# Hybrid decoder layer: output weights with folded gains, split during the projection and used in three rounded products, and attention maps normed behind the values

## What is computed

```python
h = rms_norm(x, norm1_g[l])
proj = h @ w_in[l]                                   # 512 x 3072
dq, dk, dv, rq, rk, rv, rg = jnp.split(proj, PROJ_SPLITS, axis=-1)
...
s = jnp.einsum('bqhmd,bkhmd->bhmqk', qb, k) * scale  # two maps m for each of 4 heads
s = jnp.where(causal, s, -jnp.inf)
p = jax.nn.softmax(s, axis=-1)
a = p[:, :, 0] - lam * p[:, :, 1]
out = jnp.einsum('bhqk,bkhd->bqhd', a, v)
...
d_out = rms_norm(d_out, diff_norm_g[l]) * (1.0 - lam_init)     # each head's 128 columns
r_out = rms_norm(retention(rq, rk, rv, log_decay), ret_norm_g[l])
r_out = r_out.reshape(B, S, RET_WIDTH) * jax.nn.silu(rg)
mix = jnp.concatenate([d_out.reshape(B, S, DIFF_WIDTH), r_out], axis=-1)
x = x + mix @ w_o[l]                                 # 512 x 1024 by 1024 x 1024
h2 = rms_norm(x, norm2_g[l])
x = x + moe(h2, ...)                                 # top 4 of 32 experts
out = rms_norm(x, norm_f_g)
```

## Time and profile before

| | |
|---|---|
| median of 3 runs | 1559.16 us (1559.05 to 1561.57) |
| profiled execution | 1565.79 us, its span 1563.9 us |
| PE busy in the span | 1483.7 us (95%) |
| DVE, ACT, POOL busy | 1294.1, 1009.3, 220.3 us |
| before the experts' first product | 363.8 us |

### The profile page before, as it was taken

How to read it: one execution, slowest core, us unless ns; L and a number is a source line. 1 busy time by engine, 2 the same in 40 slices (tenths; PEclk the granted TensorE clock), 3 DMA queues, 4 the chain that set the end, 5 groups by cost and what they waited for, 6 DMA issues and landing times.

```text
span 1563.9 us, 23287 instructions
## 1 busy us (share of the span) xinstructions
PE 1483.7 (95%) x7401; PEld 1237.8 (79%) x7401; DVE 1294.1 (83%) x1151; ACT 1009.3 (65%) x898; POOL 220.3 (14%) x237
## 2 busy tenths in 40 slices
PE   7999679878999999999999999999999999999993
PEld 6999458746888888888888888888888888888882
DVE  5642671458999999999999999999999999999998
ACT  5221551225777777777777777777777777777773
POOL 1000301132012111111111111111111121101111
PEclk8999798868999999999999999999999999999997
DMA  9200701016999999999999999999999999999996
GB/s 288 96 27 1 269 1 41 28 41 233 357 365 364 359 367 374 365 375 364 380 371 369 363 373 364 374 366 371 363 372 379 365 367 366 373 369 371 363 369 257
DMA packets 142278, 467.61 MB, mean 299 GB/s; under 512 B 15702, under 2 KB 32370, under 8 KB 142185
## 3 DMA queue, kind: packets, MB, share of 16 engines
q1 hardware_dynamic: 128096, 445.17, 77.3%
q0 software_dynamic: 13408, 19.88, 3.9%
q10 hardware_dynamic: 744, 2.17, 0.4%
HBM read 464.02 MB, written 21.79 MB: 311 GB/s over the span
## 4 chain that ended last, share of the span: by engine, by line
PE 90%; DVE 3%; DMA 3%; ACT 2%; issue 2%; POOL 0%; SPq 0%; POOLq 0%; DVEq 0%; ACTq 0%
PE pair L848 23%; PE pair L850 23%; PE pair L856 23%; PE pair L745 4%; PE pair L601 3%; PE pair L602 3%; PE pair L606 3%; PE pair L824 2%; PE pair L863 2%; PE pair L874 2%; DMA ring<-in_w_in 1%; DMA gain_row<-in_ret_norm_g 1%; DVE row_max L1268 1%; PE pair L767 0%; PE pair L794 0%
## 5 line engine op out<-in xcount | busy, mean ns | idle before, releaser
L1518 DVE TENSOR_TENSOR split<-ring,split 128x2048 fp32r<-128x2048 f32 x396 | 892.1, 2288 | 75.5 <-ACT split L1091 75.3
L1091 ACT CAST split<-ring 128x2048 fp32r<-128x2048 f32 x396 | 758.5, 1916 | 200.9 <-PE pair L856 192.4
L848 PE MATMUL pair<-split,operands 128*128 128x512 f32 x1584 | 631.0, 398 | 1.7 <-DVE operands L1539 1.7
L850 PE MATMUL pair<-split,operands 128*128 128x512 f32 x1584 | 618.9, 391 | 0.0
L856 PE MATMUL pair<-split,operands 128*128 128x512 f32 x1584 | 424.4, 390 | 0.0
L856 PEld LDWEIGHTS pair<-split,operands 128*128 128x128 f32 x1584 | 297.5, 188 | 63.2
L848 PEld LDWEIGHTS pair<-split,operands 128*128 128x128 f32 x1584 | 298.2, 188 | 61.3 <-issue 2.2
L850 PEld LDWEIGHTS pair<-split,operands 128*128 128x128 f32 x1584 | 298.4, 188 | 58.6
L1749 POOL DMA_INDIRECT expert_rows<-work,list_cur x33 | 44.7, 1353 | 513.9 <-PE pair L856 507.9
L1742 POOL DMA_INDIRECT work<-h_rows,token_next x35 | 74.3, 2123 | 196.9 <-DMA token_next<-slot_lists 179.5
L601 PE MATMUL pair<-split,operands 128*128 128x256 f32 x352 | 88.1, 287 | 3.4 <-DVE work L1254 3.4
(11 more groups left out here) (227 smaller groups left out, 1205.2 us busy)
## 6 DMA issues: line engine op xcount, KB each, us to landing
ring<-in_w_moe_in SPq DMA_DIRECT2D x264, 1024.0 KB, 8.0
ring<-in_w_moe_out SPq DMA_DIRECT2D x132, 1024.0 KB, 8.4
ring<-in_w_in SPq DMA_DIRECT2D x12, 1024.0 KB, 9.5
ring<-expert_rows SPq DMA_DIRECT2D x3, 2048.0 KB, 8.3
late_ring<-in_w_o SPq DMA_DIRECT2D x4, 1024.0 KB, 9.6
resid<-in_x SPq DMA_DIRECT2D x4, 512.0 KB, 5.4
h_rows<-work ACTq DMA_DIRECT2D x4, 512.0 KB, 2.7
late_ring<-expert_rows SPq DMA_DIRECT2D x4, 512.0 KB, 5.4
```

The costliest lines, as they stand in the source:

```text
L848: pe.matmul(dst[:, f, :], left_hi[:, k0 + k, :], hi[c.buffer][:, k, cols], start=(start and k == 0), stop=False)
L850: pe.matmul(dst[:, f, :], left_lo[:, k0 + k, :], hi[c.buffer][:, k, cols], start=False, stop=False)
L1091: act.copy(hi[c.buffer], raw[c.slot]).then_inc(hi_made, 1)
L1518: dve.tensor_tensor(lo[c.buffer], raw[c.slot], hi[c.buffer].bitcast(F32), ALU.subtract).then_inc(lo_made, 1)
```

## The change

Four things are done.

1. The head norms' gains are no longer rows that POOL multiplies in. They come as columns (`mix_gain`, with `g1_col` in `gain_cols`) through two small transfers on ACT's queue, and are folded into `w_o`, whose row k belongs to gain k. `N_SMALL` falls from 10 to 5.
2. `w_o` is loaded by rows (four chunks of 256 rows) as slots of the projection's ring come free, and split in the last two chunks of the projection: `w_out_hi` on ACT, `w_out_lo` on DVE. `mix` is split at its eviction too, and PE makes three rounded products, 48 of 512 columns for each tile. PE waits for the low parts of `mix` only ahead of the last third.
3. The attention maps are not divided by their sums ahead of the values: map 0 gets the second one added, times a ratio of the sums; the division by the first sum goes into the head norm (`row_rec`). The score's scale is put into the q columns of the projection (`row_scale`), and the maxima come out negated.
4. Where buffers went elsewhere, waits follow: SP loads the first expert's six chunks only after the fourth output product (`wo_done`).

```diff
-OUT_CHUNKS = D // CW
-N_SMALL = 10
+OUT_CHUNKS = KT // 2
+WO_FROM = NCHUNK - W_RAW
+N_SMALL = 5
...
+        wo_raw = [rows_of(ring[:, (WO_FROM + q) % W_RAW].rearrange("p k c -> p (k c)")) for q in range(OUT_CHUNKS)]
+        wo_lo = [rows_of(ring_split[:, (WO_FROM + q) % W_RAW]) for q in range(OUT_CHUNKS)]
+        wo_hi = [rows_of(m) for m in (ring_split[:, (NCHUNK - 1) % W_RAW], ring_split[:, W_RAW], split[:, 0], split[:, PARTS])]
...
-            for q, s in enumerate(wo_slot):
-                sp.wait_ge(proj_ready, NT * NCHUNK)
-                sp.dma_start(slot(s), w_o_cols[:, :, q * CW:(q + 1) * CW]).then_inc(wo_full[q], 16)
+            for q in range(OUT_CHUNKS):
+                sp.wait_ge(w_hi_made, WO_FROM + q + 1)
+                sp.wait_ge(w_lo_made, WO_FROM + q + 1)
+                sp.dma_start(wo_raw[q], w_o_rows[q]).then_inc(wo_full[q], 16)
...
-            sp.wait_ge(w_hi_made, NCHUNK)
-            sp.wait_ge(w_lo_made, NCHUNK)
-            sp.wait_ge(rope_done, len(ROPE_CHUNKS))
+            sp.wait_ge(wo_done, NT)
             for n in range(RAW):
                 sp.dma_start(raw[n], first_chunk(0, n)).then_inc(early_loaded, 16)
...
-                pe.wait_ge(mixT_by_act, i + 1)
-                pe.wait_ge(mixT_by_dve, i + 1)
                 if i < 2:
                     ret_output(i + 2)
...
+                dst = pair[1 + i % 2]
+                for k in range(KT):
+                    q, n = divmod(k, 2)
+                    if k % 4 == 0:
+                        pe.wait_ge(mixT_by_act, 2 * i + k // 4 + 1)
                     if i == 0:
-                        pe.wait_ge(wo_full[q], 16)
-                    dst = pair[1 + i % 2][:, q // 2, (q % 2) * CW:(q % 2 + 1) * CW]
-                    for k in range(KT):
-                        mm = pe.matmul(dst, mixT[:, i % 2, k, :], slot(s)[:, k, :],
-                                       start=(k == 0), stop=(k == KT - 1))
+                        pe.wait_ge(wo_hi_made, k + 1)
+                        pe.wait_ge(wo_lo_made, k + 1)
+                    for f in range(2):
+                        cols = slice(f * 512, (f + 1) * 512)
+                        pe.matmul(dst[:, f, :], mixT_hi[:, i % 2, k, :], wo_hi[q][:, n, cols], start=(k == 0), stop=False)
+                        pe.matmul(dst[:, f, :], mixT_hi[:, i % 2, k, :], wo_lo[q][:, n, cols], start=False, stop=False)
+                for k in range(KT):
+                    q, n = divmod(k, 2)
+                    if k % 4 == 0:
+                        pe.wait_ge(mixT_by_dve, 2 * i + k // 4 + 1)
+                    for f in range(2):
+                        cols = slice(f * 512, (f + 1) * 512)
+                        mm = pe.matmul(dst[:, f, :], mixT_lo[:, i % 2, k, :], wo_hi[q][:, n, cols],
+                                       start=False, stop=(k == KT - 1))
                 mm.then_inc(wo_done, 1)
...
+            def w_out_hi(q):
+
+                act.wait_ge(wo_full[q], 16)
+                if q == 0:
+                    act.wait_ge(w_lo_made, NCHUNK)
+                if q == 1:
+                    act.wait_ge(rope_done, len(ROPE_CHUNKS))
+                if q >= 2:
+                    act.wait_ge(proj_ready, NT * (NCHUNK - 2))
+                for n in range(2):
+                    act.activation(wo_hi[q][:, n, :], wo_raw[q][:, n, :], ACT.Copy, scale=mix_gain[:, 2 * q + n:2 * q + n + 1])\
+                        .then_inc(wo_hi_made, 1)
...
+            def w_out_lo(q):
+
+                for n in range(2):
+                    k = 2 * q + n
+                    dve.wait_ge(wo_hi_made, k + 1)
+                    dve.scalar_tensor_tensor(wo_lo[q][:, n, :], wo_raw[q][:, n, :], mix_gain[:, k:k + 1],
+                                             wo_hi[q][:, n, :].bitcast(F32), ALU.mult, ALU.subtract).then_inc(wo_lo_made, 1)
...
                     if i == 1 and c + 2 < NCHUNK:
                         w_in_lo(c + 2)
+                    if c >= NCHUNK - 2:
+                        w_out_lo(2 * (c - NCHUNK + 2) + i // 2)
...
-                chain(dve.reciprocal(row_rec[:, b, :], row_sum[:, b, :]))
-                chain.settle()
-                chain(dve.tensor_tensor(row_rec[:, b, 1:2], row_rec[:, b, 1:2], lam[:, 5:6], ALU.mult))
-                chain.settle()
-                chain(dve.tensor_scalar(probs[:, b, 1, 0:n], probs[:, b, 1, 0:n], row_rec[:, b, 1:2], None, ALU.mult))
-                chain.settle()
-                dve.scalar_tensor_tensor(probs[:, b, 0, 0:n], probs[:, b, 0, 0:n], row_rec[:, b, 0:1],
-                                         probs[:, b, 1, 0:n], ALU.mult, ALU.add).then_inc(att_ready, 1)
+                chain(dve.reciprocal(row_ratio[:, b:b + 1], row_sum[:, u, 1:2]))
+                chain.settle()
+                chain(dve.scalar_tensor_tensor(row_ratio[:, b:b + 1], row_sum[:, u, 0:1], lam[:, 5:6], row_ratio[:, b:b + 1],
+                                               ALU.mult, ALU.mult))
+                chain.settle()
+                dve.scalar_tensor_tensor(probs[:, b, 0, 0:n], probs[:, b, 1, 0:n], row_ratio[:, b:b + 1],
+                                         probs[:, b, 0, 0:n], ALU.mult, ALU.add).then_inc(att_ready, 1)
+                if u % NH == NH - 1:
+                    dve.reciprocal(row_rec[:, u // NH, :], row_sum[:, u - NH + 1:u + 1, 0]).then_inc(row_scale_ready, 1)
...
             def mix_evict(i):
-                dve.wait_ge(mix_transposed, 2 * i + 2)
-                dve.tensor_copy(mixT[:, i % 2, 4:8, :], bank[1].rearrange("p (k t) -> p k t", k=4)).then_inc(mixT_by_dve, 1)
+                for a in range(2):
+                    tiles = slice(4 * a, 4 * a + 4)
+                    dve.wait_ge(mixT_by_act, 2 * i + a + 1)
+                    dve.tensor_tensor(mixT_lo[:, i % 2, tiles, :], bank[a].rearrange("p (k t) -> p k t", k=4),
+                                      mixT_hi[:, i % 2, tiles, :].bitcast(F32), ALU.subtract).then_inc(mixT_by_dve, 1)
```

More of the change, by code:

```diff
@@ L136, in build @@
         y_dram = nc.dram_tensor("expert_rows", [SEQ * TOPK, D], F32, kind="Internal").ap()
+        with nc.sbuf_tensor("ring_split", [P, RAW, 2 * HALF], F32R) as ring_split:
+            pass
         ring = sb("ring", [P, RAW, KT, CW])
@@ L464, in after_last @@
             return eng.value_load(last_pass[0:1, 0:1], min_val=0, max_val=MAX_PASSES - 1) + 1
-        wo_slot = [RING - OUT_CHUNKS + q for q in range(OUT_CHUNKS)]
         block = ctx.enter_context(nc.Block())
@@ L1044, in mix_evict @@
             def mix_evict(i):
-                act.wait_ge(mix_transposed, 2 * i + 1)
-                act.copy(mixT[:, i % 2, 0:4, :], bank[0].rearrange("p (k t) -> p k t", k=4)).then_inc(mixT_by_act, 1)
+                for a in range(2):
+                    act.wait_ge(mix_transposed, 2 * i + a + 1)
+                    act.copy(mixT_hi[:, i % 2, 4 * a:4 * a + 4, :], bank[a].rearrange("p (k t) -> p k t", k=4))\
+                        .then_inc(mixT_by_act, 1)
             ret_squares(0)
@@ L1069, in _ @@
                 act.wait_ge(h2_transposed, 2 * i + 1)
-                act.copy(mixT[:, i % 2, 0:4, :], bank[6].rearrange("p (k t) -> p k t", k=4)).then_inc(h2T_by_act, 1)
+                act.copy(h2T[i % 2][:, 0:4, :], bank[6].rearrange("p (k t) -> p k t", k=4)).then_inc(h2T_by_act, 1)
                 if i == NT - 2:
@@ L1267, in maxima @@
                 dve.wait_ge(scores_ready, u + 1)
[L1268 to L1272 removed]
+                dve.tensor_reduce(row_bias[:, b, :], pair[b][:, :, 0:n], AX_X, ALU.max, negate=True).then_inc(bias_ready, 1)
             def difference(u):
@@ L1575, in _ @@
             x_lo(0, 1)
+            dve.wait_ge(b_in_split, 3)
             make_lo(0, 2)
@@ L1635, in _ @@
                 small.append((lam_rows[:, n, :], for_all_partitions(row[0])))
-            for h in range(NH):
-                small.append((gain_row[:, h * P:(h + 1) * P], for_all_partitions(diff_norm_g[0])))
-            small.append((gain_row[:, 512:D], for_all_partitions(ret_norm_g.rearrange("a h c -> (a h c)"))))
             assert len(small) == N_SMALL
```

98 lines of the change are left out of this document (56 added, 42 removed).

## The result

The changed kernel takes **1549.23 us** (median of 4 runs, 1548.2 to 1551.24) against 1559.17 beside it: 9.9 us less by the medians; the ratio of the runs is 0.9922 (interval 0.9907 to 0.9938), which is 12 us or 0.8%. I had said 1537 and a range of 1530 to 1546. The sign was right, the size about half of the 22 us foretold. On another chip, with more runs, it was 7.6 us by the medians and 8.3 by the ratio, 0.9947 (0.9928 to 0.9966).

A forecast was written before the change was run, and what follows sets the result against it. PE holds 90% of the chain; only the first 363.8 us change, where stage gains go straight into the time. Start -4.9, late copies +1.5, attention -7.2, output products -11.4 sum to -22.0: 1559.2 to 1537 us, range 1530 to 1546.

The forecast's parts named there:

- the first expert's weights ... Cost 0: After output product 3: the six MB land in 15 us, within the 29.4 us before ACT's first split, so cost 0.
- rival E: Ahead of the experts: late weights, at half rate 31 us, 1 to 2 us late; 1538 us; chance 0.02.
- third and fourth tile ... I take -1.5: Attention, third and fourth tile: less DVE work shortens PE's waits ahead of the map transposes, at most 2.5 us; taken -1.5.
- -1.0 there: Attention, last but one subtraction: 1.65 us beside a POOL gain product where others take 0.75; -1.0 us.
- the late pair: Projection's end: DVE's last pair of weight subtractions, 2.5 us, delays the q and k copies; +1.5 us, bounds 0.5 and 2.5.
- POOL's blocking: Attention's start: DVE instructions blocked beside POOL's work; fewer POOL multiplications take off 3 to 4 us.
- rival B: Attention: PE takes DVE's place at once, or late copies cost 2.5 us; net -1 instead of -5.7; 1542 us; chance 0.15.
- 1.4 us at router 0: Router 0: the clock falls sooner, its short products take 3.6 instead of 2.2 us; +1.4, bounds 0 and +3.
- the start: Early projection: five small transfers instead of ten shorten DVE's wait and PE's gap, keeping the clock up; -4.9 us.
- the output products: Output-product stage: 48 products a tile instead of 64 records, product 1 mostly hidden; -11.4 us, or -10.6 without product 0's wait.
- the wait ahead of router 0: After product 1: PE stands 2.4 us until DVE's normed tile, which waits for POOL, is ready.
- the two sized terms: Apparently the start, forecast at -4.9 us, and the output products, at -10.6 us.

The follow-up runs named there:

- a_once_more: The changed kernel, unchanged, profiled a further time; its attention took 75.5 us and its output products 69.9 us; no total time is given.
- a_weights: The changed kernel with only three of the first expert's six loads behind the output products, three when the lists' entries are placed; its ratio is not in the text.
- a_stores_first: The changed kernel with the first expert's six loads held back until the four stores of normed rows have landed; its ratio is not in the text.
- a_again: The changed kernel, unchanged, measured and profiled again on another chip: 1553.58 us, ratio 0.9947 to the kernel before.
- a_pool_again: The changed kernel with eight multiplications that nobody reads put back on POOL in the attention: ratio 0.9929 to the kernel before.
- a_banks: The changed kernel with the attention's four value tiles written to banks 6 and 7 in turn instead of all to bank 6: ratio 0.9886 to before.
- a_three_three: The changed kernel with three first-expert loads behind the stores of normed rows and three behind the first gather's landing; it gained nothing.
- b_loads_late: The kernel before with only the first expert's six loads held back until the last output product is done: ratio 1.0033, 5.2 us slower by the ratio.

## Why the prediction was wrong

**The failing step is "the first expert's weights ... Cost 0".** It failed twice. I asked only whether six MB land before ACT wants them ("Six MB at the 410 GB/s of rows 7 are 15 us"). They don't: they took 32.8 us in the profile after and 37.3 in a_once_more, and ACT's first split started 0.1 us behind the last landing, 3.5 us later than the tables alone would have let it (29.4 us behind product 3 in before, and in a_weights, where three loads stand there). That cost nothing by luck, since the three splits ended at 341.4 and PE got the expert's rows at 345.9. And I didn't ask what the loads do to the small transfers that the tables and the gather consist of; there the cost lies. Measured +2.5, +5.7 and +6.6 us in three executions, 0 with the loads away, +2.6 in before with them put there. My rival E had the late weights right (31 us, 1 to 2 late, against 32.8 and 3.5), at 0.02 of the chance, but put its price on them. The Trainium skill, DMA: Bandwidth & Descriptors, section "Queues, rings and completion order", says that each DMA engine takes turns between its queues packet by packet; the trace agrees in that the stores and entries aren't queued behind all six MB: in the profile after the fourth store, issued behind the six loads, landed 12 us ahead of the last of them, and in a_stores_first the last list entry, 8.05 us long, landed 5.8 us ahead. In the three profiles of the changed kernel, though, the entry, 5.2 to 8.2 us instead of 3.6, landed within 0.4 us of the last load (in a_again, of ACT's split that the load released), so what share of its wait is taking turns and what is the loads' end is open.

**The second is the attention's "third and fourth tile ... I take -1.5" and "-1.0 there".** The first tile gave 3.5 us net of the late pair in the profile after (2.3 in a_again; foretold 3.2), but not by the steps foretold: I gave 3 to 4 us of it to POOL's blocking, and with POOL's products put back (a_pool_again) the second tile's first maxima come 19.9 us behind the projection, against 18.4 and 19.6 without them and 21.9 in before. So that blocking is worth 0.3 to 1.5 us there, and the rest of the gain lies in the fewer and shorter steps. For the third and fourth I foretold -2.5 together, and in the profile after they take 11.6 and 17.0 us instead of 11.4 and 16.6: PE's waits for DVE were shortened, and its waits for ACT's squares and copy of bank 6 grew by 0.5 to 0.9 us, three times. The squares got a scale operand (0.38 to 0.40 instead of 0.29 to 0.31 us each), and PE, held less by DVE, comes to this wait sooner. This is rival B's form, another engine taking DVE's place, with ACT where I had PE; a_banks shows it by taking the wait away.

**The third is the clock.** I took the granted clock of one execution as the kernel's own, but for 1.4 us at router 0. The stage from projection to products has 0.84 in one execution of the changed kernel and 0.78 in another, and 5 us between them. Over 34 runs of before on one chip the mean clock orders the times: 0.967 with 1559 to 1561 us, 0.962 or 0.963 with 1563 to 1566. On one chip the median clock is 0.966 before and 0.961 after; at an equal 0.966, 1546 to 1549 stands against some 1561, 13 us instead of 8. By this comparison of runs, which no experiment isolates, part of what the edits won in work was given back as clock; what sets the clock of an execution is open.

**Right by their steps:** the start (-4.9; -5.2 alone, -3.7 in the means, with the gap at 0.97 us and the clock up), the late pair (+1.5; +1.6), the output products (-10.6; -10.0, three tiles on the path and one hidden), the wait ahead of router 0 (2.4; 2.81) with its slower router. Of the overall miss of 12 us against the median, 4.8 are the loads, 4.1 the attention with its clock, 1.8 the two sized terms; the rest, some 1.5, I put down to the sampling of executions, my sum having been carried from one profile to the median.

## What to carry to other kernels

A bulk load that is moved is not free because nothing on the path waits for it: list every small transfer and store on the chain in its new neighbourhood, and expect any of them to grow: beside the loads, entries took 1.1 to 2.3 times their own length here, token numbers up to 3.8, the gather up to 2.5 times. Price the bulk load, too, by what runs beside it, and not by its rate alone. When a wait on one engine is shortened, read the *second* releaser at the same place, and look whether one more buffer takes it away. Where stages run at a clock that changes, take three or four profiles of before first; a stall of 2 or 3 us that PE met at full clock cost two to three times that here (2.81 us: 7), and removing it was worth more than its length.

## What the runs showed of the hardware

- In a_three_three three MB of loads with list entries and 0.5 MB of gains beside them moved at 208 GB/s over 16.8 us, with the DMA engines 0.90 busy, against 410 where the six loads ran with nothing beside them. Six loads beside the stores and entries took 32.8 us from first issue to last landing in the profile after.
- The last of the four stores of 512 KB landed in 13.7 and 17.1 us beside the six loads (after, a_once_more), in 5.6 to 7.4 in the four profiles of before; the other three took 2.6 to 2.9 in both.
- Extra work on POOL lengthened four DVE steps by 0.7 to 1.0 us each and the kernel was nonetheless no slower (5.9 us less by the medians, 2.8 by the ratios), at a clock of 0.88 instead of 0.84 or 0.78 in that stage.
- Of the gap early in the projection, one of 3.3 to 3.4 us was followed by the low clock in three executions, one of 2.25 us in the fourth and one of 2.45 in b_loads_late weren't.
